# Gate row folded into the output weights of a Hyena/attention/expert layer on one Trainium2 core

## What is computed

```python
def _merge(y_a, y_b, gate_logits, w_branch_a, w_branch_b, w_out):
    ga, gb = jnp.split(jax.nn.sigmoid(gate_logits), 2, axis=-1)
    return (ga * (y_a @ w_branch_a) + gb * (y_b @ w_branch_b)) @ w_out
...
    x_new = x + g1 * _merge(y_a, y_b, zx[..., OFF_G:], w_branch_a, w_branch_b, w_out)
    hx2 = _rms(x_new, norm2) * (1 + sc2) + sh2
    x_new = x_new + g2 * _expert_choice(hx2, router, w_gate, w_up, w_down)
```

## Time and profile before

| | us |
|---|---|
| median of 3 runs | 2148.73 (2147.58 to 2149.17) |
| the profiled execution | 2147.46 |
| its span, first to last instruction | 2145.7 |
| PE busy in it | 2110.3 (98%) |
| DVE busy | 1682.3 (78%) |
| ACT busy | 1176.8 (55%) |
| POOL busy | 199.8 (9%) |
| mean granted TensorE clock | 0.993 |

### The profile page before, as it was taken

How to read it: one execution, slowest core, us unless ns; L and a number is a source line. 1 busy time by engine, 2 the same in 40 slices (tenths; PEclk the granted TensorE clock), 3 DMA queues, 4 the chain that set the end, 5 groups by cost and what they waited for, 6 DMA issues and landing times.

```text
span 2145.7 us, 28103 instructions
## 1 busy us (share of the span) xinstructions
PE 2110.3 (98%) x10397; PEld 1687.8 (79%) x10397; DVE 1682.3 (78%) x1821; ACT 1176.8 (55%) x1282; POOL 199.8 (9%) x86
## 2 busy tenths in 40 slices
PE   9999999989999999999999999999999999999998
PEld 4998888866678786787578888888888888888886
DVE  4667766248885999855988998889988988889986
ACT  4421222146631222334277777777777777777874
POOL 1000000000000001300010222012220222102200
PEclk9999999999999999999999999999999999999999
DMA  8134354130012135543799999999999999999993
GB/s 319 59 103 165 128 186 167 49 128 16 16 50 103 60 113 192 165 158 118 296 409 401 401 401 382 397 393 378 376 377 401 391 378 378 382 399 383 383 375 104
DMA packets 183003, 540.62 MB, mean 252 GB/s; under 512 B 14597, under 2 KB 56935, under 8 KB 182288
## 3 DMA queue, kind: packets, MB, share of 16 engines
q1 hardware_dynamic: 172872, 507.85, 62.6%
q0 software_dynamic: 5264, 17.00, 3.1%
q10 hardware_dynamic: 4792, 14.74, 1.7%
HBM read 503.90 MB, written 35.65 MB: 251 GB/s over the span
## 4 chain that ended last, share of the span: by engine, by line
PE 60%; DVE 1%; DMA 0%; issue 0%; POOL 0%; ACT 0%; POOLq 0%
PE p_y L334 5%; PE p_y L336 5%; PE p_y L335 5%; PE p_b L334 5%; PE p_b L335 5%; PE p_b L336 5%; PE p_a L336 5%; PE p_a L334 5%; PE p_a L335 5%; PE p_m L334 2%; PE p_m L336 2%; PE p_m L335 2%; PE p_t L2999 1%; PE p_a L3028 1%; PE p_m L2260 1%; PE p_t L2990 1%
## 5 line engine op out<-in xcount | busy, mean ns | idle before, releaser
L2866 DVE TENSOR_TENSOR r_lo<-ring,r_hi 128x2048 fp32r<-128x2048 f32 x372 | 838.9, 2286 | 59.0 <-ACT r_hi L2825 57.8
L2825 ACT ACTIVATE r_hi<-ring 128x2048 fp32r<-128x2048 f32 x372 | 708.3, 1916 | 148.6 <-PE p_b L336 76.4
L334 PE MATMUL p_y<-r_hi,a_hi 128*128 128x512 f32 x512 | 205.3, 401 | 0.0
L336 PE MATMUL p_y<-r_hi,a_lo 128*128 128x512 f32 x512 | 199.9, 391 | 0.0
L335 PE MATMUL p_y<-r_lo,a_hi 128*128 128x512 f32 x512 | 199.2, 389 | 0.0
L334 PE MATMUL p_b<-r_hi,x_hi 128*128 128x512 f32 x496 | 193.1, 389 | 0.0
L336 PE MATMUL p_b<-r_hi,x_lo 128*128 128x512 f32 x496 | 193.0, 389 | 0.0
L335 PE MATMUL p_b<-r_lo,x_hi 128*128 128x512 f32 x496 | 192.9, 389 | 0.0
L334 PE MATMUL p_a<-r_hi,x_hi 128*128 128x512 f32 x480 | 189.8, 395 | 0.0
L336 PE MATMUL p_a<-r_hi,x_lo 128*128 128x512 f32 x480 | 187.3, 390 | 0.0
L335 PE MATMUL p_a<-r_lo,x_hi 128*128 128x512 f32 x480 | 186.8, 389 | 0.0
(11 more groups left out here) (427 smaller groups left out, 3883.3 us busy)
## 6 DMA issues: line engine op xcount, KB each, us to landing
ring<-in_w_gate SPq DMA_DIRECT2D x128, 1024.0 KB, 10.5
ring<-in_w_up SPq DMA_DIRECT2D x128, 1024.0 KB, 9.0
ring<-in_w_down SPq DMA_DIRECT2D x128, 1024.0 KB, 12.5
w_raw<-in_w_in SPq DMA_DIRECT2D x17, 1024.0 KB, 6.2
ada_rest<-in_ada_w SPq DMA_DIRECT2D x16, 1024.0 KB, 5.4
ada<-in_ada_w SPq DMA_DIRECT2D x8, 1024.0 KB, 15.1
gate_dram<-zs ACTq DMA_DIRECT2D x16, 512.0 KB, 2.6
x_normed<-gate_dram SPq DMA_DIRECT2D x16, 512.0 KB, 4.2
```

What stands on the lines that cost most here:

```text
L334: pe.matmul(out, a_hi, b_hi, start=start, stop=False)
L336: return pe.matmul(out, a_lo, b_hi, start=False, stop=stop)
L2825: act.activation(r_hi[:, i % PARTS], ring[:, i % RAW], ACT.Copy).then_inc(hi_ready, 1)
L2866: dve.tensor_tensor(r_lo[:, i % PARTS], ring[:, i % RAW], r_hi[:, i % PARTS].bitcast(F32), ALU.subtract).then_inc(lo_ready, 1)
```

## The change

The rows of `wo` are multiplied by `g1row` in place, once each, by VectorE: `gated_weights(k)` for k = 0 to 7, 128x1024 each, stands behind `merged_low(i)` for i = 6 to 13. ScalarE waits for it (`wo_gated`) ahead of each high part. Behind the projection the product with `g1row` is gone; `new_rows` adds the bank to the x rows directly, and TensorE's waits for a free bank are on `xnew_ready` instead of `read`.

```diff
--- before.py
+++ after.py
@@ -2156,7 +2156,7 @@
         xr_in = [sem(f"xr_in{i}") for i in range(XB)]
         job, read = sem("m_job"), sem("m_read")
         mul, mt_ready, mt_hi, mt_lo = sem("m_mul"), sem("mt_ready"), sem("mt_hi"), sem("mt_lo")
-        wo_high, wo_low = sem("wo_hi_ready"), sem("wo_lo_ready")
+        wo_gated, wo_high, wo_low = sem("wo_gated"), sem("wo_hi_ready"), sem("wo_lo_ready")
         y_high, y_low = sem("y_hi_ready"), sem("y_lo_ready")
         w_high, w_low = sem("branch_hi_ready"), sem("branch_lo_ready")
         xnew_ready, sq_ready = sem("xnew_ready"), sem("sq2_ready")
@@ -2276,7 +2276,7 @@
                 if n == 0 and t < 2:
                     pe.wait_ge(read, M - 2 + t)
                 if t >= 2 and ks[0] == 0:
-                    pe.wait_ge(read, M + (2 * (t - 1) if t > 2 else 0) + n + 1)
+                    pe.wait_ge(xnew_ready, (2 * (t - 1) if t > 2 else 0) + n + 1)
                 for k in ks:
                     if t == 0 and n == 0 and k in (0, 6, 7):
                         pe.wait_ge(wo_low, max(k + 1, 6))
@@ -2350,7 +2350,7 @@
                     mm = spread_row(t)
                 elif kind == "c":
                     pe.wait_ge(minus_ready, 1)
-                    pe.wait_ge(read, M + 2 * NT - 1)
+                    pe.wait_ge(xnew_ready, 2 * NT - 1)
                     for n in range(1, t + 1):
                         mm = count_below(n)
                 elif kind == "s":
@@ -2416,6 +2416,7 @@
 
         def merge_scalar(act):
             def out_high(k, n):
+                act.wait_ge(wo_gated, k + 1)
                 act.activation(wo_hi[:, k, half(n)], wo[:, k, half(n)], ACT.Copy).then_inc(wo_high, 1)
 
             act.wait_ge(b_done, 2 * SPECTRA)
@@ -2533,6 +2534,10 @@
                 dve.tensor_tensor(wo_lo[:, k, half(n)], wo[:, k, half(n)], wo_hi[:, k, half(n)].bitcast(F32),
                                   ALU.subtract).then_inc(wo_low, 1)
 
+            def gated_weights(k):
+                dve.wait_ge(o_in, 16)
+                dve.tensor_tensor(wo[:, k], wo[:, k], g["g1row"][:], ALU.mult).then_inc(wo_gated, 1)
+
             def weighted(i):
                 b = pj[:, i % 4]
                 dve.wait_ge(job, i + 1)
@@ -2565,6 +2570,8 @@
                     for k in range(2):
                         out_low(2 * (i - KD - 4) + k, 0)
                 merged_low(i)
+                if KD - 2 <= i < 2 * KD - 2:
+                    gated_weights(i - KD + 2)
             for k in range(NO):
                 out_low(k, 1)
 
@@ -2580,10 +2587,8 @@
                 dve.wait_ge(job, n_job[("op"[n == 0], t)])
                 if t:
                     dve.wait_ge(xnew_ready, 2 * t + n - 1)
-                dve.tensor_tensor(step[:, half(n)], pj[:, rows_pair(t), n], g["g1row"][:, half(n)], ALU.mult).then_inc(read, 1)
-                dve.wait_ge(read, M + 2 * t + n + 1)
                 dve.wait_ge(xr_in[t % XB], 16 * (t // XB + 1))
-                dve.tensor_tensor(xt, xt, step[:, half(n)], ALU.add).then_inc(xnew_ready, 1)
+                dve.tensor_tensor(xt, xt, pj[:, rows_pair(t), n], ALU.add).then_inc(xnew_ready, 1)
 
             def row_root(t):
                 c = slice(t, t + 1)
```

## The result

| | before | changed |
|---|---|---|
| median of 5 runs, us | 2147.58 (2146.82 to 2149.17) | 2158.74 (2153.92 to 2159.00) |
| profiled execution, us | 2147.46 | 2158.96 |
| its span, us | 2145.7 | 2157.2 |
| PE busy, us | 2110.3 | 2115.4 |
| DVE busy, us | 1682.3 | 1681.7 |

The changed kernel is slower: ratio 1.0044, 95% interval 1.0034 to 1.0055, some 7 to 12 us. The two medians are 11.2 us apart; the ratio stands for 9.4. VectorE's busy time has hardly moved, as eight wide products replace sixteen narrow ones. Of the 11.5 us between the two profiled spans, 10.8 arise between the low part of job 6 (about 884 us) and the first gather.

The account below looks back on a forecast made before the run. TensorE was taken as the bound, busy through projection and experts, so a late projection reaches the end. Stall 7.6 + clock 1.7 - end 0.6 = +8.7 us on 2148.7 gave 2157.4, range 2154.0 to 2161.5.

Parts of the forecast that it names:

- the stall with a short low stretch: Main case: projection starts 7.6 us late, low clock behind it costs 1.7, time 2157.4 us; chance 0.72.
- the base of the sum: Median of three runs of the kernel before, 2148.7 us, to which the forecast added its +8.7 us.
- The eight products: VectorE's queue, jobs 6 to 13: 1.14 us per product, the first 1.47 because of GpSimd, 9.45 us together.
- Who waits: First projection matmul waits for the sixth low part; after 1.9 us of slack TensorE starts 7.6 us later.
- job 11: TensorE's job in the gated sum, predicted to wait 0.3 us for `read` 8, included in the 7.6 us.
- TensorE's clock: Behind the stall ahead of the projection, work at the lower clock costs 1.7 us, between nothing and 3.4.
- the stretch at 451.8: Earlier low-clock stretch, 451.8 to 455.1, granted clock 0.50, unbroken matmuls; its 1.7 us loss was taken for the stall.
- What the change takes away: Sixteen products behind the projection, 11.1 us of VectorE: fifteen worth nothing, the last -0.6 us, between -0.72 and 0.
- ScalarE's copy and the filling matmuls: End of the projection, before the first gather: said to limit the square root's gain to some 0.6 us.
- the products are hidden: Rival in VectorE's queue before the projection: idle time absorbs the products, only the tail counts, 2148.1 us; chance 0.11.
- VectorE's own saving counts whole: Rival: VectorE's saved and added time counts fully, -11.1 + 9.1 = -2.0, so 2146.7 us; chance 0.02.
- The clock costs more: Rival: low clock costs 3.4 us behind the stall and 1.7 in the experts' first matmuls, 2160.8 us; chance 0.15.

Follow-up runs that it names:

- e10: The changed kernel run again, unaltered, on the same chip as e9 and e11: 2157.30 us, ratio 1.0045.
- e1: The changed kernel without the eight products with the gate row, the single addition behind the projection kept: 2146.84 us, ratio 0.9995.
- e2: The kernel before with the eight products added, product and addition behind the projection left as they were: 2158.22 us, ratio 1.0049.
- e3: The changed kernel with products of 128x512 instead of 128x1024 in the same eight places: 2151.54 us, ratio 1.0016.
- e5: The changed kernel with each product one step earlier in VectorE's queue, between the job's sum and its low part: 2151.68 us, ratio 1.0016.
- e4: The changed kernel with 29 matmuls of 512 columns filling TensorE's stall ahead of the first projection: 2155.26 us, ratio 1.0033.
- e8: The kernel before, unaltered, run once more for a second profile of its clock: 2146.87 us.
- e6: The changed kernel with left half-products inside VectorE's wait, right ones behind the last job, first right projection waiting for low parts singly: 2147.20 us, ratio 0.9998.
- e11: The kernel of e6 run again, unaltered, on the same chip as e9 and e10: 2147.76 us, ratio 1.0000.
- e7: The changed kernel with all products moved from VectorE to GpSimd, as 16 halves, left ones first: 2155.96 us, ratio 1.0032.
- e9: The kernel of e6, but the first right projection waits for all sixteen low parts again: 2151.84 us, ratio 1.0017.

## Why the prediction was right

The forecast was the stall with a short low stretch, 2157.4 us; measured were 2158.74 and, again, 2157.30. The mechanism is the one of the forecast. That the time agrees so closely is in part luck: the base of the sum, a median of three (2148.73), was 1.2 us above the median of five (2147.58), while the sum itself was short, +8.7 against +11.2, with +9.4 by the ratio and +9.0 in e10. By the steps of the text:

- **The eight products**: 1.14 us of queue each was right to the hundredth. For the whole of them I had 9.45, measured are 9.3 (922.54 against 913.27); the difference is in job 7, where GpSimd's second subtraction held VectorE a little less long.
- **Who waits**: 7.6 us later by the text, 7.5 in the profile, 7.0 to 7.05 us of them as a wait ahead of one matmul; 0.3 came earlier, at job 11, as the text had it. Nothing further bound behind it, as worked out: the last eight low parts (ready at 932.3) made no wait. e1 and e2 show that the products in that place make the loss, e3 and e5 that it goes with their width and place.
- **TensorE's clock**: the mechanism holds (e4), the size was short. I took 1.7 us from the stretch at 451.8. The work at half speed behind the stall was 5.1 us in the changed kernel (923.2 to 928.3), so 2.5; in e2's projection, without another low stretch, the clock took 106.03 - 104.57 = 1.5, in e10's 1.9 by the same subtraction. The sum had no term for where in the wait the clock falls, and that makes the difference (see e2). The Trainium skill (TensorE: Matmul & The Clock Gate, the section on why this matters) advises against such gaps. The traces agree for the gap of 7.05 us, behind which the granted clock was 0.51.
- **What the change takes away**: I had -0.6 for the end, between -0.72 and 0. Measured are -0.8 against this profile of before (10.99 to 11.01 against 11.79; 11.15 in e1), and -0.6 against the other one, whose end is 11.62 (e8). I had taken ScalarE's copy and the filling matmuls for the bound. In the changed kernel the root comes 2.32 us after the read of the bank (1034.14 - 1031.82), before it was 3.05 (1022.78 - 1019.73): a gain of 0.73, so it was VectorE's queue. From the root to the gather it is 8.74 us before and 8.69 in the changed kernel, but 8.57 in e8, which is the kernel before: the rest is within what two executions differ by.
- **The part of the profiled difference that is not the change**: 1.5 us of the 4.0 in the projection are the second low stretch, which came by itself (e8), and 0.5 us were there before the products begin. How often such a stretch comes in the executions that the medians are made of is not shown; only the profiled ones have a trace.
- **Rivals**: "the products are hidden" is what e6 makes true by moving them; in the changed kernel the idle time was there, but behind each product's place. "VectorE's own saving counts whole" falls with e1. "The clock costs more" was half right in mechanism, in the profiled run of the changed kernel: 2.5 + 1.5 us of low clock, though its second stretch lay in the projection and not in the experts' first matmuls. From the gather to the end of the span it is 1114.2 us before and 1114.4 in the changed kernel.

## What to carry to other kernels

An operation that is moved into a stretch with idle time is free only if it stands where the engine waits; behind the wait it costs its whole length, and an average of busy time over the stretch doesn't show the difference. Work out the queue position by position up to the first operation that another engine waits for, and compare the slack there (here 1.9 us) with what is put in front of it (9.3). Splitting the work by what is needed first (left halves, right halves) and waiting for parts one by one gave the same algebra at no cost that shows (e6, e11), while handing it to an idle GpSimd did not (e7).

## What the runs showed of the hardware

- After waits of 2.40 us (e5) and 2.7 us (e9) TensorE's granted clock stayed at 2.4 GHz; after 3.08 us (e3), 5.52 us (e7) and 7.0 us (changed, e2, e10) it was at 1.2 GHz. Each is one profiled execution, and the medians of e5 and e9 are 2.5 and 1.4 us above what their traces account for. In the traces with the lower level the clock cost 1.5 us (e2) to 2.8 us (e7, 108.89 - 104.57 less the 1.5 of its second low stretch). It differed between executions with the same wait, by how much of the low stretch fell on the wait (some 4 us in e2, about 1.8 in the changed kernel).
- The low stretch near the end of the projection comes and goes between kernels that do the same there (before and e8 are the same program). It costs about 1.5 us (105.98 against 104.57 in these two). It may be part of the spread of 2.6 to 3.2 us over the runs of the kernel before; that is not shown, as only profiled executions have a trace.
- Beside a product of GpSimd, VectorE's operations with two inputs in SBUF were held up in e7 (1.66 us for the sum and 1.00 for the low part, both 0.69 alone), while the product with a PSUM input kept its 0.68 us between them.
